# Transformer and hybrid block kernel: a/g convolution blocks in pairs, decays and mask once per bank, thin weights stationary

## The reference

```python
def hybrid_mixer(h, w_in, b_forget, conv_w, conv_b, conv_ln_g, conv_ln_b, w_out):
    z = h @ w_in           # a 512, g 512, q 512, k 512, v 512, f_logit 8
    u = a * jax.nn.sigmoid(g)
    u = causal_depthwise_conv(u, conv_w, conv_b)             # 31 taps
    u = jax.nn.silu(layer_norm(u, conv_ln_g, conv_ln_b))
    log_f = jax.nn.log_sigmoid(f_logit + b_forget)
    att = forgetting_attention(q, k, v, log_f)               # 8 heads of 64
    return jnp.concatenate([u, att], axis=-1) @ w_out

# in forgetting_attention, for each block of 128 queries
    logits = q @ k.T * scale
    logits = logits + cum[:, :, q0:kl, None] - cum[:, :, None, :kl]   # cum = cumsum(log_f)
    p = softmax(where(mask, logits, -1e30)); out = p @ v
```

## Time and profile before

| | us |
|---|---|
| three runs | 1523.06, 1524.91, 1529.28 |
| their median | 1524.91 |
| the profiled execution | 1526.07 |
| its span in the profile | 1524.3 |
| mean granted clock of TensorE | 0.976 of full |
| busy: PE, DVE, ACT, POOL | 1450.7, 1061.9, 758.1, 70.4 |

### The profile page before, as it was taken

The page is one execution under the profiler, slowest core; times in us unless marked ns, Lnnn a source line. Parts: engine busy times, 40 slices in busy tenths (PEclk is TensorE's granted clock), DMA queues, the critical chain, the costliest instruction groups (busy, mean ns, idle before and its releaser), DMA issues.

```text
span 1524.3 us, 27149 instructions
## 1 busy us (share of the span) xinstructions
PE 1450.7 (95%) x9388; PEld 1312.1 (86%) x9388; DVE 1061.9 (70%) x1978; ACT 758.1 (50%) x1210; POOL 70.4 (5%) x87
## 2 busy tenths in 40 slices
PE   7999889999899998989989999999999999999997
PEld 7977679899699787779989999999999999988886
DVE  5798666555668676659997999555555555577775
ACT  5633665444557533444554555444444444444443
POOL 0200100000000531000000000000000000000000
PEclk9989999999989999999999999999999999999999
DMA  7332235555434531454535788755757566577753
GB/s 282 134 127 84 90 104 180 193 183 188 138 124 157 163 100 66 139 181 152 167 137 195 245 260 258 241 186 185 244 184 247 186 208 220 185 241 247 250 191 144
DMA packets 103209, 274.56 MB, mean 180 GB/s; under 512 B 8160, under 2 KB 41056, under 8 KB 102640
## 3 DMA queue, kind: packets, MB, share of 16 engines
q1 hardware_dynamic: 64832, 237.11, 47.2%
q10 hardware_dynamic: 38032, 34.63, 6.9%
q0 software_dynamic: 288, 2.10, 0.4%
HBM read 254.93 MB, written 18.87 MB: 180 GB/s over the span
## 4 chain that ended last, share of the span: by engine, by line
PE 83%; DVE 13%; issue 2%; ACT 2%; POOL 0%; DMA 0%; POOLq 0%; ACTq 0%; SPq 0%; DVEq 0%
PE Y L1775 42%; PE AO L1775 36%; DVE wl L936 4%; PE M L1775 3%; DVE CV L1017 2%; ACT wh L467 1%; DVE eqs L1530 1%; DVE I L1450 1%; DVE SCO L1466 1%; DVE I L1464 1%; DVE PU L1505 0%; DVE V L1472 0%; DVE V L1458 0%; DVE xn L959 0%; PE AO L1853 0%
## 5 line engine op out<-in xcount | busy, mean ns | idle before, releaser
L936 DVE TENSOR_TENSOR wl<-raw,wh 128x1024 fp32r<-128x1024 f32 x440 | 543.5, 1238 | 282.9 <-ACT wh L467 282.1
L467 ACT CAST wh<-raw 128x1024 fp32r<-128x1024 f32 x440 | 459.4, 1046 | 183.1 <-PE AO L1775 93.1
L1775 PE MATMUL AO<-xh,wh 128*128 128x256 f32 (+1 forms) x1776 | 512.6, 289 | 6.5 <-DVE wl L936 6.4
L1775 PE MATMUL AO<-xl,wh 128*128 128x256 f32 (+1 forms) x1776 | 505.6, 285 | 0.0
L1775 PE MATMUL AO<-xh,wl 128*128 128x256 f32 (+1 forms) x1776 | 505.6, 285 | 0.0
L1775 PEld LDWEIGHTS AO<-xh,wh 128*128 128x128 f32 x1776 | 341.0, 192 | 13.4 <-DVE wl L936 7.6
L1775 PEld LDWEIGHTS AO<-xl,wh 128*128 128x128 f32 x1776 | 339.8, 191 | 4.6
L1775 PEld LDWEIGHTS AO<-xh,wl 128*128 128x128 f32 x1776 | 340.9, 192 | 0.0
L1775 PE MATMUL Y<-wh,peer_ah 128*128 128x512 f32 x512 | 200.8, 392 | 2.1 <-DVE peer_al L1592 2.1
L1775 PE MATMUL Y<-wh,peer_al 128*128 128x512 f32 x512 | 200.3, 391 | 0.0
L1775 PE MATMUL Y<-wl,peer_ah 128*128 128x512 f32 x512 | 199.2, 389 | 0.0
(11 more groups left out here) (301 smaller groups left out, 1724.7 us busy)
## 6 DMA issues: line engine op xcount, KB each, us to landing
raw<-in_stream SPq DMA_DIRECT2D x440, 512.0 KB, 3.3
gate_spill<-gstage ACTq DMA_DIRECT2D x32, 512.0 KB, 5.1
gates<-gate_spill ACTq DMA_DIRECT2D x6, 2048.0 KB, 15.2
gates<-gate_spill ACTq DMA_DIRECT2D x8, 512.0 KB, 7.1
rowg<-in_post SPq DMA_DIRECT2D x3, 512.0 KB, 4.7
X<-in_x SPq DMA_DIRECT2D x2, 512.0 KB, 4.7
memx<-in_mem SPq DMA_DIRECT2D x1, 1024.0 KB, 8.3
keys<-in_keys POOLq DMA_DIRECT2D x1, 1024.0 KB, 6.8
```

The source lines that it names most:

```text
L467: nc.scalar.copy(wh[:, s, :], raw[:, s, :]).then_inc(split_hi, 1)
L936: nc.vector.tensor_tensor(wl[:, s, :], raw[:, s, :], wh[:, s, :].bitcast(F32), ALU.subtract)\
L1775: return nc.tensor.matmul(o, a, b, start=start, stop=stop)
```

## The change

Four things are done in one program.

- **a/g blocks in pairs.** `AG_ORDER` loads the blocks as a0, g0, a1, g1 and so on. ScalarE takes the sigmoid of a g tile as it evicts it; VectorE forms `UP` of each tile in the ag stage and does four taps behind each split there from the fourth on, 20 in all. The order of the taps starts with ten taps on tiles 0 and 1 and ends with ten on tiles 2 and 3. Behind each v split stand 5 taps, in an attention step 8 (`TAPS`), and the taps end at s = 6.
- **End of the convolution.** `row_sums(0, CV)` stands ahead of the last mv block, not behind it; the last low part and the last mk split stand behind the subtraction of the mean; the squares are taken inside step 7.
- **Thin products.** The thin weights are now stationary (8 or 24 columns), 24 matmuls of 256 or 272 columns each. ScalarE copies the product out of its bank (`thin_copy`) and TensorE turns it (`thin_turn`) behind qk block 0 and behind xbc block 2; the xbc product itself moves ahead of block 2.
- **Logits.** The decays and the mask are one matmul each per bank of 512 columns (in "second" groups `ones` has a matmul of its own with 256), ahead of the q times k products.

Besides, evictions that only copy are written as `copy`.

The diff, cut to its core:

```diff
-TAPS = 9
+TAPS = 8
+AG_ORDER = (0, 4, 1, 5, 2, 6, 3, 7)
...
+        thin_t = at("thin_t", [SSD_H, TM], 8 * THIN, base=choice_at)
...
-                sp.dma_start(raw[:, s, :], stream[s]).then_inc(landed[s], 16)
+                sp.dma_start(raw[:, s, :], stream[AG_ORDER[s]]).then_inc(landed[s], 16)
...
+                    held = AG_ORDER[b0 + s] if b0 + s < 8 else b0 + s
+                    sp.dma_start(raw[:, s, :], stream[held]).then_inc(landed[s], 16)
...
+                if func is ACT.Copy and type(scale) is float and scale == 1.0:
+                    nc.scalar.copy(dest, AO[:, e % 2, 0:n]).then_inc(a_free, 1)
+                else:
+                    nc.scalar.activation(dest, AO[:, e % 2, 0:n], func, scale=scale).then_inc(a_free, 1)
...
+            def thin_copy(i, width, n):
+                act.wait_ge(thin_prod, i + 1)
+                nc.scalar.copy(thin_t[0:width, 0:n], M[0:width, 1, 0:n]).then_inc(thin_out, 1)
...
-                evac("ag", j, AG[:, j, :])
+                k = AG_ORDER[j]
+                evac("ag", j, AG[:, k, :], func=ACT.Copy if k < CT else ACT.Sigmoid)
                 split(STREAM["ag"] + 4, j)
-            act.wait_ge(a_free, 8)
-            nc.scalar.activation(AG[:, CT:, :], AG[:, CT:, :], ACT.Sigmoid).then_inc(gate_sig, 1)
...
+                if j == 0:
+                    thin_copy(0, FOX_H, T)
...
+                    act.wait_ge(dec_done, 3)
+                    act.wait_ge(ln_xc, 1)
+                    nc.scalar.activation(SQ[:, :, :], CV[:, :, :], ACT.Square).then_inc(ln_sq, 1)
                 split(STREAM["mk"] + 4, s)
                 if 2 <= s < 7:
                     values_high(s - 2)
                 if 1 <= s < 7:
                     turned_back(s - 1)
 
-            act.wait_ge(dec_done, 3)
-            act.wait_ge(ln_xc, 1)
-            nc.scalar.activation(SQ[:, :, :], CV[:, :, :], ACT.Square).then_inc(ln_sq, 1)
...
+                if j == 1:
+                    thin_copy(1, SSD_H, TM)
...
-            split_ahead(STREAM["ag"], 8)
-
-            dve.wait_ge(gate_sig, 1)
-            nc.vector.tensor_tensor(UP[:, :, CONV_W - 1:], AG[:, 0:CT, :], AG[:, CT:, :], ALU.mult)\
-                .then_inc(conv_pad, 1)
-            dve.wait_ge(conv_pad, 2)
-
-            taps = [(w, c) for w in range(CONV_W) for c in range(CT)]
+            BOTH = 10
+            taps = [(w, c) for w in range(BOTH) for c in (0, 1)]
+            taps += [(w - (BOTH if c > 1 else 0), c) for w in range(BOTH, CONV_W) for c in range(CT)]
+            taps += [(w, c) for w in range(CONV_W - BOTH, CONV_W) for c in (2, 3)]
+            tap_at = {t: k for k, t in enumerate(taps)}
+            seen = [0]
...
+                    dve.wait_ge(conv_pad, c + 2)
...
+                need = tap_at[w - 1, c] + 1
+                if need > seen[0]:
+                    then = taps[min(k + 1, len(taps) - 1)]
+                    then = tap_at[then[0] - 1, then[1]] + 1 if then[0] else 0
+                    seen[0] = max(need, then) if then <= k - 1 else need
+                    dve.wait_ge(conv_step, seen[0])
...
+            for j in range(8):
+                split(STREAM["ag"] + 4, j)
+                if j % 2:
+                    c = j // 2
+                    dve.wait_ge(a_free, 2 * c + 2)
+                    nc.vector.tensor_tensor(UP[:, c, CONV_W - 1:], AG[:, c, :], AG[:, CT + c, :], ALU.mult)\
+                        .then_inc(conv_pad, 1)
+                if j >= 3:
+                    some_taps(4)
...
-                some_taps(6)
+                some_taps(5)
...
-            some_taps(len(taps))
-            dve.wait_ge(conv_step, len(taps))
-            nc.vector.tensor_copy(stat[:, 14:15], CV[:, 0, 0:1]).then_inc(conv_done, 1)
-            values_low(FOX_GROUPS - 1)
-            split(STREAM["mk"] + 4, 7)
+                if s == 6:
+                    some_taps(len(taps))
+                    dve.wait_ge(conv_step, len(taps))
+                    nc.vector.tensor_copy(stat[:, 14:15], CV[:, 0, 0:1]).then_inc(conv_done, 1)
 
             v = UP[:, 0, 0:T]
             dve.wait_ge(ln_sum, 1)
             nc.vector.scalar_tensor_tensor(out=CV[:, :, :], in0=AO[:, 0, 0:T][:, None, :].to_broadcast([P, CT, T]),
                                            scalar=-1.0 / CONV_CH, in1=CV[:, :, :], op0=ALU.mult,
                                            op1=ALU.add).then_inc(ln_xc, 1)
+            values_low(FOX_GROUPS - 1)
+            split(STREAM["mk"] + 4, 7)
...
-            def thin(outs, at, width):
-
+            def thin(at, width, n):
+
+                o = M[0:width, 1, 0:n]
+                for kt in range(KT):
+                    e = slice(at + width * kt, at + width * kt + width)
+                    mm(o, thin_h[:, e], xh[:, kt, 0:n], kt == 0, False)
+                    mm(o, thin_l[:, e], xh[:, kt, 0:n], False, False)
+                    ins = mm(o, thin_h[:, e], xl[:, kt, 0:n], False, kt == KT - 1)
+                ins.then_inc(thin_prod, 1)
+
+            def thin_turn(i, outs, width):
+
+                pe.wait_ge(thin_out, i + 1)
                 for o, r, c in outs:
-                    for kt in range(KT):
-                        e = slice(at + width * kt, at + width * kt + width)
-                        for n, (part, w) in enumerate(((xh, thin_h), (xh, thin_l), (xl, thin_h))):
-                            ins = mm(o, part[:, kt, c:c + r], w[:, e], kt == 0 and n == 0, kt == KT - 1 and n == 2)
+                    ins = nc.tensor.transpose(o, thin_t[0:width, c:c + r], ident[0:width, 0:width])
                 return ins
...
-            thin([(M[:, 0, 8 * j:8 * j + 8], P, P * j) for j in range(TT)],
-                 0, FOX_H).then_inc(f_prod, 1)
+            thin(0, FOX_H, T)
             for j in range(8):
                 wide("qk", j, xh, xl, T)
+                if j == 0:
+                    thin_turn(0, [(M[:, 0, 8 * j:8 * j + 8], P, P * j) for j in range(TT)], FOX_H).then_inc(f_prod, 1)
...
+                kind, e, m = groups[g]
                 if g >= 2:
                     pe.wait_ge(at_exp, g - 1)
+                n, w = len(members(g)), members(g)[0][2]
+                o = M[:, g % 2, :].rearrange("p (n k) -> p n k", n=n)
+                if kind != "mem":
+                    d = DEC[:, :, :, :].rearrange("p (a e) n k -> p e a n k", e=2)[:, e, 2 * m:2 * m + n, :, :]
+                    if kind == "first":
+                        mm(o, upper[:, :], d[:, :, 0, :], True, False)
+                    else:
+                        mm(o, upper[:, :], d[:, :, 1:3, :].rearrange("p a n k -> p a (n k)"), True, False)
+                        mm(o[:, :, 0:P], ones[:, :], d[:, :, 0, :], False, False)
+                    mm(o[:, :, w - P:], ident[:, :], mask[:, None, :].to_broadcast([P, n, P]), False, False)
                 for i, (h, j, w) in enumerate(members(g)):
-                    o = M[:, g % 2, w * i:w * i + w]
                     if kind == "mem":
-                        ins = mm(o, MQ[:, h, P * j:P * j + P], MK[:, h, :], True, True)
-                        continue
-                    r = slice(FOX_D * (h % 2), FOX_D * (h % 2) + FOX_D)
-                    mm(o, QK[r, h // 2, P * j:P * j + P], QK[r, CT + h // 2, 0:w], True, False)
-                    if j == 0:
-                        mm(o, upper[:, :], DEC[:, h, 0, :], False, False)
+                        ins = mm(o[:, i, :], MQ[:, h, P * j:P * j + P], MK[:, h, :], True, True)
                     else:
-                        mm(o[:, 0:P], ones[:, :], DEC[:, h, 0, :], False, False)
-                        mm(o, upper[:, :], DEC[:, h, 1:3, :].rearrange("p a b -> p (a b)"), False, False)
-                    ins = mm(o[:, w - P:w], ident[:, :], mask[:, :], False, True)
+                        r = slice(FOX_D * e, FOX_D * e + FOX_D)
+                        ins = mm(o[:, i, :], QK[r, h // 2, P * j:P * j + P], QK[r, CT + h // 2, 0:w], False, i == n - 1)
...
+            def row_sums(bank, src):
+                for c in range(CT):
+                    ins = mm(AO[:, bank, 0:T], ones[:, :], src[:, c, :], c == 0, c == CT - 1)
+                ins.then_inc(ln_sum, 1)
+
             for s in range(8):
                 if s < FOX_GROUPS:
                     logits(s)
+                if s == 7:
+                    pe.wait_ge(a_free, A_BASE["mk"] + 4)
+                    pe.wait_ge(conv_done, 1)
+                    row_sums(0, CV)
...
-            pe.wait_ge(a_free, A_BASE["mk"] + 4)
-            pe.wait_ge(conv_done, 1)
-            row_sums(0, CV)
...
-            for j in range(1, 4):
-                wide("xbc", j, xh, xl, TM)
-            thin([(M[0:META, 0, 0:24], META, 0)] + [(M[:, 0, 24 * (j + 1):24 * (j + 2)], P, META + P * j)
-                                                    for j in range(TT)],
-                 KT * FOX_H, SSD_H).then_inc(dt_prod, 1)
+            wide("xbc", 1, xh, xl, TM)
+            thin(KT * FOX_H, SSD_H, TM)
+            wide("xbc", 2, xh, xl, TM)
```

(3 more changed lines are left out.)

20 lines of the change are left out of this document (6 added, 14 removed).

## The result

| | before | changed |
|---|---|---|
| median of six runs, us | 1523.99 | 1515.59 |
| lowest to highest | 1519.96 to 1529.28 | 1515.26 to 1517.03 |
| profiled execution (span) | 1526.07 (1524.3) | 1515.26 (1513.5) |

The ratio is 0.9943 with a 95% interval of 0.9928 to 0.9959: 8.4 us by the medians, 10.8 between the two profiled executions, where the forecast had 13.65. The sign and the range (1505 to 1519) are right, the likeliest value (1511.3) is 4.3 too low. One execution of 3889 us (of the kernel before, in a later series) and one of 8011 us (of e10) are left out of the ratios.

What follows compares the result with a forecast made beforehand. TensorE, busy 95%, was taken as the bound except where VectorE leads. Gains 1.65 + 1.6 + 3.0 + 3.0 + 4.4 = 13.65 took 1526.07 to 1512.4 us, on the median 1511.3; range 1505 to 1519.

Steps and rivals of the forecast that it cites:

- The bound: Whole kernel: TensorE, busy 95% of the span, except where VectorE leads, from about 60 us to the first softmax product.
- (a): Thin forget gate and its turn: cheaper product and low-clock stretch gone, 4.0 us, less 2.35 for wait and transposes: 1.65.
- (b): Taps in the a/g stage: 20 taps cost nothing there, VectorE's row before the first softmax product 1.6 us shorter.
- (c): Attention logits, decays and mask once per bank: 3.0 us gained, from groups 2 to 5.
- The clock at 99 us: Behind the wait before the first softmax product: TensorE still 2.6 us early, so the low clock was kept there.
- the clock falls less often: Rival: block qk 3, group 2 and block mk 2 gain 5.6 us more, 1505.7 us; chance 0.16.
- The rival of the low clock: Rival: clock stays low around the thin products and row sums, gain only 6.95, 1518.0 us; chance 0.22.
- (d): End of the convolution, sixth peak to w_out: 16.7 us instead of 19.7, gain 3.0; 1.2 with row sums at 3.57.
- (e): Time-step thin product: 5.6 us won with the low clock behind it gone, 1.35 back for ScalarE's lateness: gain 4.4.
- The median: Whole kernel: the gain of 13.65 us, summed on the profiled 1526.07, was carried over to the median 1524.91, giving 1511.3.

Runs made afterwards that it cites:

- e10: Changed kernel with the forget gate's turn behind qk block 1 and 6 taps moved from the v splits to behind the last ag split: 1511.65 us, ratio 0.9909.
- e6: Changed kernel with 13 taps moved from the v splits to behind the last ag split (6) and qk split 0 (7): 1507.32 us, ratio 0.9887.
- the control: The changed kernel run once more, unchanged: 1514.40 us, ratio 0.9937 to the kernel before.
- e2: Kernel before with the convolution's changes alone (pairs, sigmoid at eviction, taps, end of the convolution): 1518.84 us, ratio 0.9966.
- e1: Kernel before with the two thin products alone changed (stationary weights, copy, turn): 1524.56 us, ratio 0.9998.
- e9: Kernel before with the thin products alone changed and the turn behind qk block 1: 1520.86 us, ratio 0.9966.
- e3: Kernel before with the logits alone changed (decays and mask once per bank): 1522.65 us, ratio 0.9989.
- e7: Changed kernel with the thin products as before, the other parts kept: 1518.84 us, ratio 0.9956.

## Why the prediction was right or wrong

The time lies in the range that was forecast, and that was in part luck. Two terms that the forecast counted brought little by themselves, and a clock gain that it had put at nothing made up for them.

- **The bound** was read rightly: VectorE's row from 60 us to the first softmax product. That it goes on to the second values at 113 us was missed; the chain of e6 runs through VectorE up to 108.7 us.
- **(a)** Forecast 1.65. The profiled pair shows 0.9 at 61, against the other three executions with the old thin product (-2.5, -2.7, -3.0) some 3 to 4: in those the clock fell during the product, which took 6.9 to 7.4 us instead of 5.4. The new product was sized well (2.78 us against 2.84), and so was the wait (2.12 against 1.9), but the wait's cause is partly another than put down: the memory's scaling kept ScalarE until 43.7 us. The step that failed is "The 1.2 GHz stretch behind goes too, 4.35 - 2.84 = 1.5": it moved behind the new wait, as long as it was (47.0 to 50.4 us, in the control 45.6 to 49.0), and TensorE reaches the memory's transposes at 54.80 us against 54.18 before (the thin product began 0.9 later, behind a longer low stretch at 13 us). The 0.9 comes from the other stretch: "I also keep the 4.40 us block behind it at the low clock" did not hold, that block ran at full clock in the pair and in the control, which is worth the same 1.5. That a part of the wait hangs on the sigmoid's place was not seen.
- **(b)** Forecast 1.6, measured 1.6 (2.5 - 0.9). Right, and small beside what was there: 6 us of idle VectorE at 42 and 48 us. "So they cost nothing" asked whether 20 taps fit, not how many more would.
- **(c)** Forecast 3.0; alone 1.7 us (0.9989), beside the convolution 1.0 at full clock, from groups 4 and 5 (forecast 1.1 for the two). The price of a first group was right in sum: 2.90 against 4 x (0.42 + 0.33 + 0.31) = 4.24 before (1.3 less, 1.08 forecast) because 512 columns cost 0.86 and 0.95 but the q-k products fell from 0.42 to 0.27 us each. A second group went from 3.22 to 2.87, 0.35 less where 0.54 was forecast. The step that failed is "Group 2 is at the low clock ... group 3 gives 1.0": once the low stretch was gone VectorE led up to the second values, and both groups gave nothing.
- **The clock at 99 us.** "So I keep the low clock behind it": between 98 and 132 the changed kernel won 4.7, of which e2, with the old logits, has 3.6. From the first att_p to the second values before needed 19.8 us and the changed kernel 16.1, and this 3.7 paid for (c). Before had a low stretch there, which the rows put at 7.1 us and which lasts 10.2 (99.7 to 109.9 us); e1 and e9 have it as long, no kernel with the convolution's part has it, and where 3.4 us of it came back, in the control, it cost nothing. This is the rival "the clock falls less often", here in part. Why the stretch goes with the convolution's part stays open.
- **The rival of the low clock** rested on "four of four waits or thin stretches of over 2 us had it". The trace of before has waits of 2.49 us at 503.87 and of 2.21 at 616.65 with full clock behind them, and the changed kernel has low stretches behind both.
- **(d)** Forecast 3.0, measured 2.5 (9.7 - 7.2). 16.8 us from the sixth peak (124.35) to wout (141.15), forecast 16.7: it was before's 19.3 that was put at 19.7. Of the 2.5, 1.6 is the row sums at full clock, which e1, e3 and e9 have without this part (17.7 us from peak to wout); the new end of the convolution itself is worth 0.9, where "at the 3.57 of before it is 1.2".
- **(e)** Forecast 4.4 (5.6 - 1.35 would be 4.25), measured 3.6 in the pair (12.5 against 8.9 at 410 us), 3.7 in e1. TensorE was 5.6 us further ahead at 444 us, as forecast; ScalarE's lateness took back 1.6 by 454 us (1.35 forecast), 1.02 of it as one wait. And 1.0 to 1.3 goes back between 457 and 560 in every kernel with the new time-step product and in none of the four without (before, e2, e3, e7): behind the same wait of 2.49 us, at 491 us, the clock now falls. A low stretch taken away at 440 us is matched by a shorter one 50 us later in all of them; what ties the two together is not shown. The forecast counted stretches removed and had no term for new ones.
- **The median.** Of the 4.3 us between 1511.3 and 1515.6, 2.8 is the gain that the pair lacks (10.8 of 13.65). 1.16 is that the gain, added up on an execution slower than the median, was taken off the median, and 0.3 that the changed kernel's profiled execution stood below its own.

The sum of the pair: 0.9 + 1.6 + 4.7 + 2.5 - 0.8 (155 to 410 us: two low stretches of 6.8 us in both, of which less falls into a wait now) + 3.6 - 1.1 - 0.8 + 0.2 = 10.8.

## What to carry to other kernels

A short operation that needs another engine's answer must be laid against that engine's whole queue, and one block of distance (the turn behind block 1, not 0) may be worth as much as the operation. Where one engine's row leads, look first for its own idle times ahead of that row: 13 taps moved there brought 3.8 us more by 560 us, in a change of three numbers. Low-clock stretches are not saved by removing one cause: price them as a gain with a chance, and take the stage table of several executions, not one. A kernel that leaves a stage alone tells what the clock gave there: e1 gained 1.6 us at row sums that it had not touched.
